# Expert stage of a two-block network: gathering two pairs of experts at a time, straight into feature layout

## The reference, cut to what matters

```
def expert_choice_moe(h, w_router, w_gate, w_up, w_down):
    cap = EC_CAPACITY_FACTOR * S // N_EXPERTS                       # 64
    affinity = jax.nn.softmax((h @ w_router).astype(jnp.float32), axis=-1)
    gate, idx = lax.top_k(jnp.swapaxes(affinity, 1, 2), cap)
    x_in = jax.vmap(lambda hb, ib: hb[ib])(h, idx)                  # 16 x 64 x 1024
    a = jnp.einsum('becd,edf->becf', x_in, w_gate)                  # 1024 -> 512
    u = jnp.einsum('becd,edf->becf', x_in, w_up)
    y = jnp.einsum('becf,efd->becd', jax.nn.silu(a) * u, w_down)    # 512 -> 1024
    y = y * gate[..., None].astype(y.dtype)
    return jax.vmap(lambda ib, yb: jnp.zeros((S, D), yb.dtype).at[ib.reshape(-1)].add(yb.reshape(-1, D)))(idx, y)
```

## Time and profile before

| | us |
|---|---|
| median of three runs (2494.99 to 2499.69) | 2499.26 |
| the profiled execution, its own time | 2494.92 |
| its span, from the first to the last instruction | 2492.9 |
| PE busy | 2390.5 (96%) |
| DVE busy | 1379.6 (55%) |
| ACT busy | 929.1 (37%) |

### The profile page before, as it was taken

The page is one execution under the profiler, slowest core; times in us unless marked ns, Lnnn a source line. Parts: engine busy times, 40 slices in busy tenths (PEclk is TensorE's granted clock), DMA queues, the critical chain, the costliest instruction groups (busy, mean ns, idle before and its releaser), DMA issues.

```text
span 2492.9 us, 29194 instructions
## 1 busy us (share of the span) xinstructions
PE 2390.5 (96%) x11260; PEld 1703.7 (68%) x11260; DVE 1379.6 (55%) x2322; ACT 929.1 (37%) x1545; POOL 221.1 (9%) x176
## 2 busy tenths in 40 slices
PE   8999997999998999889998999999999999999998
PEld 6654865444485568544447778888887778888886
DVE  5775645233558655623335565777633565777722
ACT  4486543111337754511114223444323223444421
POOL 2301203000122011200000002000001001100000
PEclk9999998999999999989999999999999999999999
DMA  4100416999620024299993212333334212323231
GB/s 172 60 1 16 141 55 218 395 394 394 252 76 26 1 67 145 82 349 394 394 397 131 69 59 85 103 100 93 102 95 143 76 51 93 92 94 98 89 110 51
DMA packets 132728, 359.24 MB, mean 144 GB/s; under 512 B 12016, under 2 KB 13040, under 8 KB 132336
## 3 DMA queue, kind: packets, MB, share of 16 engines
q1 hardware_dynamic: 132304, 356.96, 40.6%
q10 hardware_dynamic: 288, 0.42, 0.0%
HBM read 355.24 MB, written 2.10 MB: 143 GB/s over the span
## 4 chain that ended last, share of the span: by engine, by line
PE 89%; DVE 6%; ACT 3%; issue 1%; POOL 1%; DMA 0%; POOLq 0%; SPq 0%; DVEq 0%; ACTq 0%
PE ps L1152 11%; PE ps L1154 10%; PE ps L1153 10%; PE ps L1406 9%; PE ps L1428 5%; PE ps L1167 4%; PE ps L1169 4%; PE ps L1168 4%; PE ps L1311 3%; PE ps L1284 3%; PE ps L1186 3%; PE ps L1292 3%; PE ps L1187 2%; PE ps L1188 2%; PE ps L1368 1%; PE ps L1369 1%
## 5 line engine op out<-in xcount | busy, mean ns | idle before, releaser
L2134 DVE TENSOR_TENSOR wlo<-stage,whi 128x1024 fp32r<-128x1024 f32 x268 | 337.9, 1266 | 310.7 <-ACT whi L1551 310.4
L1152 PE MATMUL ps<-hTh,whi 128*128 128x512 f32 x1136 | 453.1, 399 | 0.0
L1154 PE MATMUL ps<-hTh,wlo 128*128 128x512 f32 x1136 | 443.2, 390 | 0.0
L1153 PE MATMUL ps<-hTl,whi 128*128 128x512 f32 x1136 | 443.0, 390 | 0.0
L1551 ACT ACTIVATE whi<-stage 128x1024 fp32r<-128x1024 f32 x268 | 281.5, 1056 | 339.9 <-PE ps L1169 132.0
L1152 PEld LDWEIGHTS ps<-hTh,whi 128*128 128x128 f32 x1136 | 213.8, 188 | 49.0 <-issue 4.7
L1153 PEld LDWEIGHTS ps<-hTl,whi 128*128 128x128 f32 x1136 | 213.7, 188 | 47.3 <-issue 4.3
L1154 PEld LDWEIGHTS ps<-hTh,wlo 128*128 128x128 f32 x1136 | 213.7, 188 | 45.3
L2044 DVE TENSOR_TENSOR ps<-ps,Rs 128x512 f32<-128x512 f32 x124 | 86.1, 699 | 152.9 <-PE ps L1154 142.4
L1850 POOL TENSOR_TENSOR st<-st,c 128x4 f32<-128x4 f32 (+2 forms) x47 | 59.8, 1273 | 915.3 <-DVE st L2053 732.1
L2262 DVE TENSOR_REDUCE st<-ps 128x1 f32<-128x512 f32 (+1 forms) x160 | 101.1, 632 | 66.1 <-PE ps L1284 64.0
(11 more groups left out here) (356 smaller groups left out, 4517.3 us busy)
## 6 DMA issues: line engine op xcount, KB each, us to landing
stage<-in_wpk SPq DMA_DIRECT2D x268, 512.0 KB, 3.6
wt<-in_wg SPq DMA_DIRECT2D x48, 512.0 KB, 11.7
stage<-in_wd SPq DMA_DIRECT2D x48, 512.0 KB, 12.4
ws<-in_wu SPq DMA_DIRECT2D x44, 512.0 KB, 11.4
ws<-in_wg SPq DMA_DIRECT2D x40, 512.0 KB, 11.5
wt<-in_wu SPq DMA_DIRECT2D x40, 512.0 KB, 11.6
wq<-in_wd SPq DMA_DIRECT2D x28, 512.0 KB, 12.6
wt<-in_wd SPq DMA_DIRECT2D x24, 512.0 KB, 11.3
```

Of the source, the lines that this page charges most:

```text
L1152: pe.matmul(o, h, ah, start=k == 0, stop=False)
L1153: pe.matmul(o, h, al, start=False, stop=False)
L1154: t = pe.matmul(o, lo, ah, start=False, stop=k == 7)
L2134: ve.tensor_tensor(M.wlo[i % NW][:, :], M.stage[i % NSTAGE][:, :], f(M.whi[i % NW][:, :]), ALU.subtract).then_inc(*S.wlo.mark(("w", i)))
```

## The change

- `xtok` transposes `hTh` and `hTl` (gain in, row factor not) instead of `x`: 16 groups of four blocks, three of them ahead of the affinities' transpose, and ACT copies each straight to `xnh` or `xnl`, reading PSUM in pairs of interleaved features. `xtm`, `xsplit` and POOL's part are gone.
- `gather(g)` serves two pairs: the token-major block is the loaded operand and `Sel` for four experts (256 columns) the streamed one, so the result is feature-major. 64 products of 256 columns for two pairs; ACT copies to `xin`. `xg`, `xturn` and its copies are gone. It runs after `gate_up` of pairs 1, 3 and 5.
- The row factor enters in the activation: `gate` fetches it beside the affinity (6 columns instead of 4), ACT's tanh and DVE's product take it as a scale.
- Places: `topk` reads PSUM in its first round; `work` is turned to token-major, the mask is made there, and the places come from four fp32 products (`count`) with a triangular matrix (`upto`) and ones. The softmax takes the maximum before the row factor is there.
- `nstat` of this stage sums two tiles (`nacc` up to block 6 and the last square), eight small fp32 products instead of four, and POOL's last addition is gone.
- Weights: gate and up chunks are one run of 4 KB for each partition (features 2p and 2p + 1 in partition p), 27 buffers in another order, 7 early chunks. The eight `turned` chunks wait until `xtok` is done.
- The last pair's `down` is done half by half, each with its own `yout`.

The planner and the layout:

```diff
+        for i in range(13, 17):
+            self.do("eload", l, i, ("start",))
...
         self.do("nstat", 3 * l + 2, u2)
         self.drop(u2)
         for j in range(NSTAGE):
-            load("split", self.limit - NSTAGE + j)
-        for _ in range(2):
-            load("router")
+            self.do("eload", l, 3 + j, ("split", self.limit - NSTAGE + j))
+        for j in range(17, 19):
+            self.do("eload", l, j, ("router",))
         self.do("logits", l, u, i)
         self.drop(u)
         u = self.take()
         self.do("lg_turn", l, u)
-        self.do("point", "turned", l)
-        for _ in range(8):
-            load("turned")
         self.do("softmax0", l, u)
         self.drop(u)
+        parts = [(p, m, half) for m in range(NT) for p in range(2) for half in range(2)]
+
+        def xtok(k):
+            for p, m, half in parts[:k]:
+                u = self.take()
+                self.do("xtok", l, p, m, half, u)
+                self.drop(u)
+            del parts[:k]
+        xtok(1)
+        self.do("exp", l)
+        xtok(2)
         u = self.take()
         self.do("softmax1", l, u)
+        xtok(len(parts))
+        self.do("point", "turned", l)
+        for j in range(19, NS):
+            self.do("eload", l, j, ("turned",))
+        u2 = self.take()
...
         self.drop(u)
...
+        self.drop(u2)
+        u2 = self.take()
+        self.do("count", l, u2)
+        self.drop(u2)
+
+        def gather(g):
+            for kc in range(4):
                 u = self.take()
-                self.do("xtok", l, m, half, u)
+                self.do("gather", l, g, kc, u)
                 self.drop(u)
-            self.do("xsplit", l, m)
-        u = self.take()
...
+        def turn_sel(j):
+            for i in (j, j + 1):
                 u = self.take()
-                self.do("xturn", l, j, half, u)
+                self.do("selT", l, i, u)
                 self.drop(u)
...
+            for hs in (((0,), (1,)) if j == 7 else ((0, 1),)):
+                for k in range(4):
+                    a = self.ecur + 2 * k
+                    self.do("expert2", l, j, k, hs, Y, a)
+                    if 1 in hs:
+                        used(a)
+                        used(a + 1)
+                for h in hs:
+                    self.do("yout", l, j, h, Y[h])
+                    self.drop(Y[h])
+            self.ecur += 8
...
-        turn(0)
         for j in range(8):
-            if j < 7:
-                self.do("select", l, j + 1)
+            if j in (1, 3, 5):
+                self.do("select", l, (j + 1) // 2)
             gate_up(j)
-            if j < 7:
-                gather(j + 1)
-            tact(j)
-            if j < 7:
-                turn(j + 1)
-            if j > 0:
+            if j in (1, 3, 5):
+                gather((j + 1) // 2)
+                tact(j)
                 scatter(j - 1)
+            elif j == 0:
+                turn_sel(0)
+                tact(0)
+            else:
+                scatter(j - 1)
+                tact(j)
+                if j < 7:
+                    turn_sel(j)
             down(j)
...
-        self.slots = [early + wq + [self.stage[(38 * (l + 1) + i) % NSTAGE] for i in range(NSTAGE)] + wr + wt
-                      for l in range(2)]
+        ws = at("ws6", OC + 1408, [128, 1024])
+        self.slots = [early[0:3] + [self.stage[(38 * (l + 1) + i) % NSTAGE] for i in range(NSTAGE)] + early[3:] + [ws] +
+                      wq + wr + wt for l in range(2)]
...
-            return (wg, wu)[s][l, 2 * j + e, kc * 256:(kc + 1) * 256, :].rearrange("(k p) n -> p k n", p=128)
+            return (wg, wu)[s][l, 2 * j + e, kc * 256:(kc + 1) * 256, :].rearrange("(p k) n -> p (k n)", p=128)
...
             o = claim(u)
-            q.wait_ge(*S.pool.at("nacc", ns, 7))
+            q.wait_ge(*S.pool.at("nacc", ns, 6 if SRC[ns][0] == "moe" else 7))
+            parts = [M.nacc]
+            if SRC[ns][0] == "moe":
+                q.wait_ge(*S.act.at("nsq", ns, 7))
+                parts.append(M.nsq[1])
             for m in range(NT):
-                t = pe.matmul(o[:, m:m + 1], M.nacc[:, m * 128:(m + 1) * 128], M.one, start=True, stop=True)
+                for i, x in enumerate(parts):
+                    t = pe.matmul(o[:, m:m + 1], x[:, m * 128:(m + 1) * 128], M.one, start=i == 0, stop=i == len(parts) - 1)
             t.then_inc(*S.pe.mark(("nstat", ns)))
```

PE:

```diff
+        elif name == "count":
             l, u = a
             o = claim(u)
-            q.wait_ge(*S.dve.at("cum", l))
-            for m in range(NT):
-                t = pe.transpose(o[:, m * 16:(m + 1) * 16], M.cum[:, m * 128:(m + 1) * 128], M.ident[0:16, 0:16])
-            t.then_inc(*S.pe.mark(("cum_turn", l)))
+            mask = M.mask[:, :, :].rearrange("p m e -> p (m e)")
+            q.wait_ge(*S.dve.at("upto", l))
+            q.wait_ge(*S.pool.at("ones", l))
+            q.wait_ge(*S.dve.at("mask", l))
+            pe.matmul(o[:, 0:64], M.upto[:, :], mask, start=True, stop=False, skip_group_check=True)
+            for m in range(1, NT):
+                t = pe.matmul(o[:, 16 * m:64], M.ones[:, :], mask[:, 0:64 - 16 * m], start=False, stop=m == NT - 1,
+                              skip_group_check=True)
+            t.then_inc(*S.pe.mark(("count", l)))
         elif name == "xtok":
-            l, m, half, u = a
+            l, p, m, half, u = a
             o = claim(u)
             for i in range(4):
-                f_ = 4 * half + i
-                q.wait_ge(*S.dve.at("x", 3 * l + 2, f_))
-                t = pe.transpose(o[:, i * 128:(i + 1) * 128], M.x[:, f_, m * 128:(m + 1) * 128], M.ident)
-            t.then_inc(*S.pe.mark(("xtok", l, m, half)))
+                x = operand(("moe", l), 4 * half + i)[p][:, m * 128:(m + 1) * 128]
+                t = pe.transpose(o[:, i * 128:(i + 1) * 128], f(x), M.ident)
+            t.then_inc(*S.pe.mark(("xtok", l, p, m, half)))
...
         elif name == "gather":
-            l, j, half, u = a
-            o = claim(u)[:, :]
-            q.wait_ge(*S.dve.at("select", l, j))
-            c = slice(half * 512, half * 512 + 512)
-            for m in range(NT):
-                q.wait_ge(*S.act.at("xnh", l, m))
-                q.wait_ge(*S.pool.at("xnl", l, m))
-                pe.matmul(o, M.Sel[j % 2][:, m, :], M.xnh[:, m, c], start=m == 0, stop=False)
-                t = pe.matmul(o, M.Sel[j % 2][:, m, :], M.xnl[:, m, c], start=False, stop=m == NT - 1)
-            t.then_inc(*S.pe.mark(("gather", l, j, half)))
...
+            for kk in range(2):
+                c = slice(kc * 256 + kk * 128, kc * 256 + kk * 128 + 128)
+                for m in range(NT):
+                    q.wait_ge(*S.dve.at("select", l, g, m))
+                    for p, x in enumerate((M.xnh, M.xnl)):
+                        q.wait_ge(*S.act.at("xtok", l, p, m, kc // 2))
+                        t = pe.matmul(o[:, kk * 256:(kk + 1) * 256], x[:, m, c], M.Sel[:, m, :], start=m == 0 and p == 0,
+                                      stop=m == NT - 1 and p == 1)
+            t.then_inc(*S.pe.mark(("gather", l, g, kc)))
```

ACT, SP and DVE:

```diff
         elif name == "xtok":
-            l, m, half, u = a
-            q.wait_ge(*S.pe.at("xtok", l, m, half))
-            q.wait_ge(*S.pool.at("npow", 3 * l + 2))
+            l, p, m, half, u = a
+            q.wait_ge(*S.pe.at("xtok", l, p, m, half))
+            q.wait_ge(*S.pe.at("point", "router", l))
             all_before(q, S, "moe", l)
-            copy(M.xtm[:, m, half * 512:half * 512 + 512], M.ps[u[0]][:, :], ("xtok", l, m, half), ("free",) + u,
-                 scale=M.st[:, m:m + 1])
-        elif name == "xsplit":
-            l, m = a
-            q.wait_ge(*S.pe.at("point", "router", l))
-            q.wait_ge(*S.act.at("xtok", l, m, 1))
-            copy(M.xnh[:, m, :], M.xtm[:, m, :], ("xnh", l, m))
+            o = (M.xnh, M.xnl)[p][:, m, half * 512:half * 512 + 512].rearrange("p (c k r) -> p c k r", c=2, k=2)
+            x = M.ps[u[0]][:, :].rearrange("p (c r k) -> p c k r", c=2, k=2)
+            copy(o, x, ("xtok", l, p, m, half), ("free",) + u)
         elif name == "gather":
-            l, j, half, u = a
-            q.wait_ge(*S.pe.at("gather", l, j, half))
-            if j:
-                q.wait_ge(*S.pe.at("xturn", l, j - 1, 1))
-            copy(M.xg[:, half * 512:half * 512 + 512], M.ps[u[0]][:, :], ("xg", l, j, half), ("free",) + u)
+            l, g, kc, u = a
+            q.wait_ge(*S.pe.at("gather", l, g, kc))
+            if g:
+                q.wait_ge(*S.pe.at("gu", l, 2 * g - 1, 1))
+            copy(M.xin[:, :, 2 * kc:2 * kc + 2, :].rearrange("p b k s -> p k b s"),
+                 M.ps[u[0]][:, :].rearrange("p (k b s) -> p k b s", k=2, b=2), ("xin", l, g, kc), ("free",) + u)
...
                 q.wait_ge(*S.dve.at("hact", l, j - 1))
-            copy(M.th[:, :], M.ps[G[0]][:, :], ("th", l, j), f=ACT.Tanh, scale=0.5)
+            q.wait_ge(*S.dve.at("gate", l, j))
```

(45 more changed lines are left out.)

203 lines of the change are left out of this document (73 added, 130 removed).

## The result

The changed kernel takes 2478.01 us (median of four runs, 2477.38 to 2479.24) where the kernel before takes 2499.20 (2494.99 to 2499.69) on the same chip: a ratio of 0.9924, 95% interval 0.9913 to 0.9936. The forecast was 2480.5 us. The profiled execution takes 2477.93 with a span of 2476.1, so 16.8 us of span have gone where the sum said 18.8.

What follows compares the result with a forecast made beforehand. PE, busy 96% of the span, was taken as the bound, with transfers nearly full. 8.8 in the pairs plus 0.6 at the end gave 9.4 a layer, 18.8 in all: 2499.3 to 2480.5 us, range 2470 to 2489.

Steps and rivals of the forecast that it cites:

- loading rival: New gather's operand loads not hidden: slower if a product costs above 0.157 us; fully bare 77 more, 2558; chance 0.03.
- Eight pairs: Gate and up of pair 0 to the last down, 235.9 us before: 227.1 after, 8.8 less in a layer.
- Row statistics: Start of the expert stage: eight products instead of four, 0.80 us more; exponential 0.3 later, first maximum 0.4 earlier.
- Places: From the end of the top-k rounds to the gather: 2.9 us instead of 4.84, with 1.2 for the four fp32 products.
- First gather: Gather ahead of pair 0: 9.9 us including 2.2 lost to the low clock, 10.6 with two gates; gate and up start unchanged.
- The end: From the last down to x: one ACT copy leaves the chain, 0.6 us less in a layer.
- Weights at nothing: Weight transfers in the pairs: 1.28 us a chunk; even at the old 32.0 the reserve suffices; cost nothing.
- transfers take over: Rival: 4 KB runs bring nothing, PE waits 2 to 5 us at the end of each layer: 2485 to 2491; chance 0.10.
- DMA at 405 to 410 throughout: Sign expected in the changed kernel's profile: DMA windows at 405 to 410 GB/s throughout.
- Clock back earlier: Rival: new transposes and products keep or restore 2.4 GHz for the first gather, up to 2.2 us more a layer: 2476; chance 0.15.
- Slow copies: Rival: ACT's xtok copies from every second PSUM column take double 0.60, gather waits 1.5 us a layer: 2483.5; chance 0.15.
- another stage that moved: Sign of being wrong in the changed kernel's profile: a stage other than this one moves; no size given.

Runs made afterwards that it cites:

- the experiment: The changed kernel with the row statistics as before (POOL's last addition back, four products instead of eight): 2482.3 us, ratio 0.994.
- early splits: The changed kernel with the next mixer's three weight splits ahead of the last pair's down: 2471.67 us; run again, 2472.43 beside 2481.83 for the changed kernel.
- all edits: The changed kernel with the row statistics as before, early splits, and 58, 3 and 6 unread transposes in three top-k pauses: 2464.04 us, ratio 0.9871.

## Why the prediction was right, and where its terms were not

*How near, and how much of it is luck.* Of the 18.8 us said, the trace shows 16.7 in the two stages. The medians moved by 21.2 on one chip and by 13.5 on another, so that the first lies 2.5 from the forecast is partly luck; the ranges of 2476 to 2485 and 2470 to 2489 held on both.

*Range and mechanism held.* Gather straight to features for two pairs at once took 7.7 us out of the eight pairs of each layer. That is read from the chains and the table; no run takes the gather back alone. Products of `Sel` stand 0.12 apart (64 in 7.86), no load lies bare, so the loading rival falls. The Trainium skill (TensorE: Matmul & The Clock Gate, section LDWEIGHTS) gives a load its columns / 1.2 GHz, by estimate 107 ns for 128 columns; that is less than the 0.12 from product to product, and the trace agrees.

*Eight pairs, said 8.8, measured 7.7.* The term is mis-sized in small steps: two pairs take 59.60 instead of 59.3 (gate and up of pair 2 to that of pair 4, 481.06 to 540.66), since the gates of 6 columns take 0.79 for two pairs and not 0.68, and tact 0.52 and not 0.44. The bare waits are 0.8 in pair 0 and 0.9 in pair 7 (1.1 and 0.8 said); the second ends with DVE's additions of scatter(6), from which down takes its bank, and not with hT.

*Row statistics.* 0.8 said, 0.90 measured by the experiment. The first maximum still came 0.78 nearer to their start, more than the 0.4 said: the affinities' transpose took 0.62 where it had taken 1.03, because the clock did not fall in this stretch (1.00 from 397 to 399, 0.50 before the change). PE's new transposes ran ahead of it, where before PE stood.

*Places.* From the end of the rounds (409.47 + 0.75) to the gather 2.9 said, 414.07 - 410.22 = 3.85 measured. The count is the step: "I take 1.2 with the wait", between 0.58 and 1.6, and it takes 1.88, beyond the upper end. That end came from records of one column, and these stream 16 to 64. With the clock at 1.00 it takes 1.06. *First gather:* 10.6 said with its gates, 10.1 measured, as the clock came back during it. The rounds ended 0.3 earlier than said. These errors, +0.95, -0.5 and -0.3, nearly cancel, so gate and up of pair 0 starts where it was said to; that is luck.

*The end, 0.6:* 0.59 by the table and 0.57 by undoing it. But what I named beside it, "then splits", was the larger part of that stretch. The chain of before already went from the copies through DVE to x, and I priced only the copy.

*Weights at nothing.* This holds only with the 4 KB runs. The sentence that the old 32.0 us "uses up the reserve" and "no more" is wrong: with 2 KB runs PE waits about 2 us in the last pair of each layer, and with early splits the transfers cost 8.7. The rival "transfers take over" had the right place, the last pair, and the right mechanism. It did not occur, because its condition (4 KB runs bring nothing) was not met: the windows show 410 GB/s beside 386. What speaks for its 2 to 5 us a layer is what the 2 KB runs cost.

*DMA at 405 to 410 throughout:* not quite. It holds from 438 us on, but the queue stood until gate and up of pair 0 freed a buffer (3 GB/s from 420 to 426).

*Clock back earlier:* in part. The first gather took 9.29 against 7.86 of a later one, so 1.4 was lost there and not the 2.2 that were kept in the sum. But the count and the first 3 us of the gather still ran at 0.50, and with the count about the whole 2.2 was lost.

*Slow copies:* no. ACT's copies out of every second column, eight each:

```profile
L1540 ACT ACTIVATE xnl<-ps 128x512 fp32r<-128x512 f32 x8 | 4.7, 652 | 0.9 <-PE ps L1376 0.9
L1540 ACT ACTIVATE xnh<-ps 128x512 fp32r<-128x512 f32 x8 | 4.6, 633 | 2.0 <-PE ps L1376 2.0
```

633 and 652 ns against 0.60 of a plain copy, a tenth more at most and hidden. The Trainium skill's rule on PSUM lines (SBUF — State Buffer, section Door 1: The DMA port swizzle) speaks of matmuls; for ACT's reads this trace does not bear it out.

*Not foreseen:* the time between the stages and behind the second is not constant, and "another stage that moved" was one of the signs of being wrong. In the profiled pair it gave 1.67 and took 1.47. The gain by medians is 21.2 us on one chip and 13.5 on another; that the clock after pauses makes this difference is likely from the heads above, but not shown. What makes the clock fall after one pause and not after another of the same length stays open.

*Two slips in the sums.* By the chances given, all cases but the last and loading add up to 0.90, not 0.93. The seventh early chunk is put at 0.8 us of transfers, where the prediction's own figure for a chunk at 410 GB/s is 1.28; neither changes the forecast.

## What to carry to other kernels

When a shorter stage is forecast, price the transfers at their old rate as a real case: an edit that is worth nothing alone (4 KB runs in the old kernel) can be the condition of the gain of what it comes with. Read a chain's last pieces one by one, also those that the change leaves alone: three splits of 3.5 us stood between the last product and x, had their data some microseconds earlier, and moving them gave 3.7 us in a layer, beside 8.3 of the whole change. A wait that goes in an in-order queue is replaced by the next late operand (hT by hact) unless that is early too.

## What the runs showed of the hardware

Some microseconds without products can cost more than themselves: the granted clock falls to 0.50 (1.2 GHz) and comes back while the next work runs. A pause of 6.4 us in the rounds cost 0.8 in the count (1.88 against 1.06) and 1.2 in the gather (9.29 against 8.14). A pause of 2.5 to 3.6 us ahead of the second mixer head cost 0, 1.5 or 4.8 us from one execution to the next. Transposes of the identity, whose results nothing reads, held the clock at 1.00 where they ran; in layer 2 of the run with 56 of them it still fell behind them (0.77 and 0.66), with fillers in the next pauses too (all edits) it did not, in either layer. Where a stretch keeps DVE and ACT as its bound (the first head, 13.2 us with either clock), the low clock costs nothing. A gate or up chunk as one run of 4 KB instead of two of 2 KB moves 410 GB/s instead of 386 (385 in the changed kernel with 2 KB runs).
